# Layer 0's mixed tokens stay in token order, its output projection takes every fourth column as its weights, and one product is issued later

## The chip, the cores and the metric

The kernel runs on one core of one Trainium2 chip. A core has a matrix engine (TensorE, PE in the profile; its weight loads are shown apart, as PEld), three elementwise engines (VectorE or DVE, ScalarE or ACT, GpSimd or POOL), and SyncE (SP), which here only starts DMAs. The engines run side by side and wait for one another through semaphores. The metric is the device time of one execution in microseconds (us), the median over several runs. The kernel before takes 1310.74 us (3 runs, 1310.58 to 1311.07).

## The reference, cut to what matters

Two layers of a decoder, on 1024 tokens of width 1024, in float32:

```
def swa_sink_mixer(h, pos, w_in, sinks):                       # layer 0
    q, k, v, gate = split_cols(h @ w_in, ...)
    o, _ = banded_attention(rope(q), rope(k), v, 127, sinks)
    return o.reshape(B, S, MIX_WIDTH) * jax.nn.silu(gate)

x = x + mixer(rms_norm(x, norm)) @ w_out                       # both layers; then a last rms_norm
```

Layer 1's mixer is the same with three dilated patterns (1, 4 and 16), merged by their softmax denominators. What matters here is `mixer(...) @ w_out` of layer 0: a product of 1024 tokens x 1024 channels with a 1024 x 1024 matrix.

## The kernel before, in words

**Products.** Every float32 operand of a large product is split into two parts, `hi` (rounded) and `lo` (the rest), and three matmuls (hi hi, hi lo, lo hi) stand for one. Activations lie transposed in `ht[0]` (hi, `ht_hi`) and `ht[1]` (lo, `ht_lo`): 128 channels on the partitions, 8 channel tiles `kt`, 1024 tokens in a row of each. For an output block of 128 tokens the 128 token columns of `ht` are the stationary operand (loaded by LDWEIGHTS, PEld) and the weight rows `w_hi`, `w_lo` stream past (MATMUL, PE). In the profile such a matmul reads `j_bank<-w_hi,ht_hi`: the last name is the stationary one.

**Layer 0's tail.** The attention output of three of the four head groups was stored to `mix_dram`; it comes back through SP's queue in six loads into `qk` (three buffers), each 128 channels x 1024 tokens. The last group is still in `xr` (called `ot` in the code). Each of these eight tiles is split: ScalarE copies it into `ht_hi` (`mix_split`, L1473), VectorE subtracts to get `ht_lo` (L1825). Layer 1 wants its tokens by class (token number modulo 4), so in layer 0 this split also reorders: `mixed_from` reads the tile with a step of 4 floats, `mixed_to` writes it as four runs of 256. The last group's two tiles are first multiplied by the softmax coefficients (`end_product`, L1809, whose `qs` operand comes back from DRAM in a DMA) and by the gate (`end_mix`, L1821).

**The output projection** (jobs `("out", layer, c)`) has 8 token blocks k and three column parts c: 384, 256 and 384 columns. Part 0 goes kt by kt over eight PSUM banks (`early_rows`, `later_row`), so that it can begin before all tiles are split; its first two tiles are worked on between the last attention units. Parts 1 and 2 go block by block, 24 matmuls each. Each part and block takes 8 x 3 matmuls, so the projection of layer 0 has 3 x 8 x 24 = 576 matmuls: 384 of 384 columns and 192 of 256. `block_positions` picks the 128 token columns; before, they are contiguous for layer 0, and with a step of 2 for the third pattern of layer 1 (`s.p == 2`).

**Order.** Every engine's program is written out by hand. VectorE's work at the end of a layer comes in this order: the max of the last units, the split of tile 1 (L1825), the stores of probabilities (`empty_turn`, `probs_t<-t_bank`, L792) that TensorE's last `o_bank<-probs_t,v` (L1305) waits for, the store of the attention output (`store_ot`, L1734), the coefficients, then the other splits with the rest of the last group's mixing.

Of the kernel before, what the change touches and what calls it, by code (L numbers as in the profile page):

```python
# [7 lines left out]
F32 = mybir.dt.float32  # L8
F32R = mybir.dt.float32r
I32 = mybir.dt.int32  # L10
ALU = mybir.AluOpType
ACT = mybir.ActivationFunctionType

P = 128
# [101 lines left out]
def columns(job):  # L116
    return out_width(job[2]) if job[0] == "out" else {"qkv": QKV, "gate": R * HD}[job[0]]


def out_width(c):  # L120

    return OUT_AT[c + 1] - OUT_AT[c]
# [17 lines left out]
def half_slot(n, half):  # L140

    return (2 * n + half) % 3
# [90 lines left out]
def by_class(s):  # L233

    return s.layer == 1 and s.p == 0
# [17 lines left out]

def block_positions(view, s, n):

    if s is not None and s.p == 2:
        start = 256 * (n % 4) + n // 4
        return view[:, start:start + 2 * (P - 1) + 1:2]
    return view[:, n * P:(n + 1) * P]
# [9 lines left out]
def filled_from(view, s):  # L269

    return view.rearrange("a (e n i) -> a e n i", e=2, n=NB) if by_class(s) else view


def mixed_to(view, layer):

    return view.rearrange("a (e i) -> a e i", e=4) if layer == 0 else view


def mixed_from(view, layer):

    return view.rearrange("a (i e) -> a e i", e=4) if layer == 0 else view

# [126 lines left out]
def trunk(nc, x, positions, gains, sinks_0, final_norm, w_qkv, w_gate, w_out, out):  # L411
    ctx = ExitStack()
    with ctx:
        def sb(name, shape, dt=F32):
            return ctx.enter_context(nc.sbuf_tensor(name, shape, dt))

        def sem(name):
            return ctx.enter_context(nc.semaphore(name))
# [5 lines left out]
        ht = [sb("ht_hi", [P, KT, S], F32R), sb("ht_lo", [P, KT, S], F32R)]  # L424
# [100 lines left out]
        def gate_of(layer, g):  # L525

            return ot[0] if layer == 0 and g == GROUPS - 1 else gate

        def weights(job, part, kt):

            return w_split[part][:, half_slot(JOB[job], kt // 4), kt % 4, 0:columns(job)]

        def quarter(n, q, part):

            return w_split[part][:, half_slot(n, q // 2), 2 * (q % 2):2 * (q % 2) + 2, 0:columns(JOBS[n])]

        def raw_quarter(n, q):
            return w_raw[:, q % 2, :, 0:columns(JOBS[n])]
# [46 lines left out]
        mix_hi = sem("mix_hi")  # L585
        mix_lo = sem("mix_lo")
# [62 lines left out]
        def groups_before(t):  # L649
            return sum(s.ends_group for s in STEPS[:t])  # L650
# [8 lines left out]
        def sum_links(layer):  # L659

            return 1 if layer == 0 else 5


        def end_links(layers):

            return sum(2 * sum_links(n) + 2 for n in range(layers))
# [13 lines left out]
        def out_region(s):  # L680

            return (s.t - s.p) % 4
# [454 lines left out]
        def _(pe):  # L1137
# [32 lines left out]
            def operands(job, k):  # L1170

                if job[0] == "gate":
                    r, half = k // 2, k % 2
                    return (lambda i, kt: weights(job, i, kt)[:, r * P:(r + 1) * P],
                            lambda i, kt: ht[i][:, kt, half * 512:(half + 1) * 512], 512)
                s = STEPS[job[1]] if job[0] == "qkv" else None
                return (lambda i, kt: block_positions(ht[i][:, kt, :], s, k),
                        lambda i, kt: weights(job, i, kt), columns(job))
# [145 lines left out]
            for layer in (0, 1):  # L1324
# [32 lines left out]
                last = steps[-1]  # L1357
# [26 lines left out]
        def _(act):  # L1384
# [82 lines left out]
            def mix_in_split(layer, k):  # L1467

                act.wait_ge(mix_back[k % 3], 16 * (layer * 2 + k // 3 + 1))
                mix_split(layer, k, mix_in[k % 3])  # L1470

            def mix_split(layer, k, src):
                act.activation(mixed_to(ht[0][:, k, :], layer), mixed_from(src, layer), ACT.Copy).then_inc(mix_hi, 1)  # L1473

            def square(k, n):
                row_ready(k)(act, n)
# [45 lines left out]
            for layer in (0, 1):  # L1522
# [52 lines left out]
                last = steps[-1]  # L1575
# [41 lines left out]
        def _(dve):  # L1617
            def w_lo(quarters):
                for n, q in quarters:
                    if q % 2 == 0:  # L1620
                        dve.wait_ge(w_hi_done, 4 * n + q + 1)
                        dve.tensor_tensor(quarter(n, q, 1), raw_quarter(n, q), quarter(n, q, 0).bitcast(F32),
                                          ALU.subtract).then_inc(w_lo_done["v"], 1)
# [80 lines left out]
            def empty_turn(s, u):  # L1704
                if u % 2 == 1:
                    store_turn(dve, dve.tensor_copy, s, u).then_inc(turn_empty["v"], 1)
# [29 lines left out]
            def link(ins, sem_, value):  # L1736
                ins.then_inc(sem_, 1)
                dve.wait_ge(sem_, value)

            def coefs_first(s, k):  # L1740

                rs = coef_calls(s)[k]
                n = links_before(s.t) + k * links_per_group(s.layer)
                dve.wait_ge(exped, UNITS * s.t + NB * (rs[-1] + 1))
                if groups_before(s.t) > 0:

                    before = [q for q in STEPS[:s.t] if q.ends_group][-1]
                    dve.wait_ge(turned, TURN.filled(("C", before.t, len(coef_calls(before)) - 1)))
                at = comb_of(0, s, rs)
                if s.layer == 0:  # L1750
                    sinks = neg_sink[:, R * s.g + 2 * rs[0]:R * s.g + 2 * rs[-1] + 2]
                    sinks = sinks.rearrange("p (r o j) -> p r o j", o=1, j=2).broadcast_to([P, len(rs), NB, 2])
                    link(dve.tensor_tensor(at[:, :, 0, :, :], stat_of(s, rs, 0, 2), sinks, ALU.subtract), den_v, n + 1)
                    return
                dve.wait_ge(nat_in, 64 * (s.g + 1))
                least = comb_small[:, 0, rs[0]:rs[-1] + 1, :, :]
                link(dve.tensor_tensor(least, nat_of(0, rs, 0, 2), nat_of(1, rs, 0, 2), ALU.min), den_v, n + 1)
                link(dve.tensor_tensor(least, least, stat_of(s, rs, 0, 2), ALU.min), den_v, n + 2)
                for p in range(3):
                    of = stat_of(s, rs, 0, 2) if p == 2 else nat_of(p, rs, 0, 2)  # L1760
                    last = dve.tensor_tensor(at[:, :, p, :, :], least, of, ALU.subtract)
                link(last, den_v, n + 3)
# [37 lines left out]
            def end_product(s, r, p):  # L1800

                dve.wait_ge(ot_stored, 4 * s.t + 2 * r + 2)
                tile, by = ot[(out_region(s) + p) % 4][:, r, :], coef_end[r][p]
                if s.layer == 1:
                    tile = tile.rearrange("a (r i f) -> a f r i", r=4, f=2)
                    by = by.rearrange("p (f n i) -> p f n i", f=2, n=4)
                dve.wait_ge(end_in[3 * r + p], 32 * (1 + (s.layer == 1 and p == 0)))
                done = end_links(s.layer) + r * (sum_links(s.layer) + 1) + max(1, 2 * p)
                link(dve.tensor_tensor(tile, tile, by, ALU.mult), end_mixed, done)  # L1809


            def end_mix(s, r):

                done = end_links(s.layer) + r * (sum_links(s.layer) + 1) + 1
                into = ot[out_region(s)][:, r, :]
                for p in range(1, 1 if s.layer == 0 else 3):
                    end_product(s, r, p)
                    done += 2
                    link(dve.tensor_tensor(into, into, ot[(out_region(s) + p) % 4][:, r, :], ALU.add), end_mixed, done)
                dve.wait_ge(silued, groups_before(s.t) + 1)  # L1820
                link(dve.tensor_tensor(into, into, gate_of(s.layer, s.g)[:, r, :], ALU.mult), end_mixed, done + 1)  # L1821

            def mix_split(layer, k, src):
                dve.wait_ge(mix_hi, layer * (MIX_LOADS + 2) + k + 1)
                dve.tensor_tensor(mixed_to(ht[1][:, k, :], layer), mixed_from(src, layer),  # L1825
                                  mixed_to(ht[0][:, k, :], layer).bitcast(F32), ALU.subtract).then_inc(mix_lo, 1)

            def square(k, n):
                row_ready(k)(dve, n)
# [147 lines left out]
            for layer in (0, 1):  # L1977
# [57 lines left out]
                                coef_copy(s, 0)  # L2035
                last = steps[-1]
                coefs_first(last, 1)
                end_product(last, 0, 0)
                empty_turn(last, UNITS - 1)
                store_ot(last, 1, 1)  # L2040
                coefs_last(last, 1)
                for k in range(2, MIX_LOADS):
                    mix_split(layer, k, mix_in[k % 3])
                    if k == 2:
                        coef_copy(last, 1)
                    if k == 4:
                        w_lo(END_SPLIT[layer])
                        end_mix(last, 0)
                for k in range(2):
                    mix_split(layer, MIX_LOADS + k, ot[out_region(last)][:, k, :])  # L2050
# [82 lines left out]
```

## Time and profile before

| | |
|---|---|
| median of 3 runs | 1310.74 us |
| the profiled execution | 1306.06 us, its span 1304.3 us |
| TensorE busy | 97% of the span, granted clock 0.998 |
| VectorE, ScalarE, GpSimd busy | 59%, 49%, 28% |
| chain that ended last | TensorE 85% (L1162, the products, 59% in `j_bank` alone) |

The page gives for each engine its busy time and share of the span. The chain that ended last is followed back from the last instruction; a line's share of it is what it holds of the path that sets the end. A timeline gives instructions in order of time, with the idle time before one and who ended it. A busy TensorE need not be one at its peak: its instructions overlap, so the pace is read from the starts. Layer 0's tail with its output projection lies at about 341 to 442 us of the span.

### The profile page before, as it was taken

The numbers are of one execution on the slowest core, as the hardware profiler recorded it, in microseconds if no ns is written. First come the engines' busy times: TensorE is split into PE (matmuls) and PEld (weight loads), VectorE is DVE, ScalarE is ACT, GpSimd is POOL, SyncE is SP. The second block draws the span as 40 slices with busy tenths as digits, with TensorE's granted clock in tenths as the row PEclk, the third lists the DMA queues.
The fourth block names the chain that finished last, engine by engine and source line by source line (L and its number), as shares of the span: only waits on it lengthen the run. The fifth ranks groups of instructions, "written<-read, shape, count | busy, mean of one in ns | idle before, by whom it ended". The sixth has DMA issues, their size and how long they took to land.

```text
span 1304.3 us, 24577 instructions
## 1 busy us (share of the span) xinstructions
PE 1268.8 (97%) x8714; PEld 1182.7 (91%) x8714; DVE 763.3 (59%) x2339; ACT 643.5 (49%) x1777; POOL 368.9 (28%) x427
## 2 busy tenths in 40 slices
PE   4999999999999999999999999999999999999997
PEld 4998998988799999999989999899999899987997
DVE  5745453554772545666546666456775466668825
ACT  6445354454751445555446555456554456555312
POOL 2311142140301021212214932215832118610110
PEclk9999999999999999999999999999999999999999
DMA  5101012031546202101112311202310213215723
GB/s 203 39 19 50 26 54 85 18 98 37 173 148 202 98 25 54 40 25 25 51 50 65 86 58 36 65 26 83 98 44 19 65 39 91 84 31 138 212 98 129
DMA packets 101223, 97.29 MB, mean 75 GB/s; under 512 B 30704, under 2 KB 87536, under 8 KB 101104
## 3 DMA queue, kind: packets, MB, share of 16 engines
q1 hardware_dynamic: 101104, 95.73, 24.5%
q8 instruction: 71, 1.16, 0.4%
q14 instruction: 48, 0.39, 0.1%
HBM read 79.46 MB, written 16.25 MB: 73 GB/s over the span
## 4 chain that ended last, share of the span: by engine, by line
PE 85%; DVE 5%; issue 4%; DMA 3%; ACT 1%; SPq 1%; POOL 1%; DVEq 0%; ACTq 0%; POOLq 0%
PE j_bank L1162 59%; PE o_bank L1305 7%; PE t_bank L1284 6%; PE s_bank L1271 5%; PE j_bank L1249 3%; PE s_bank L1273 2%; DMA w_raw<-in_w_qkv 1%; PE o_bank L1162 1%; PE t_bank L1162 1%; DMA gate<-in_positions 1%; PE s_bank L1162 1%; DVE xr L1809 1%; DVE probs L1658 1%; DMA w_raw<-in_w_out 1%; DVE probs L1651 0%
## 5 line engine op out<-in xcount | busy, mean ns | idle before, releaser
L1162 PE MATMUL j_bank<-w_hi,ht_hi 128*128 128x384 f32 (+1 forms) x1312 | 445.0, 339 | 4.3 <-ACT v L1418 2.4
L1162 PE MATMUL j_bank<-w_lo,ht_hi 128*128 128x384 f32 (+1 forms) x1312 | 432.8, 330 | 0.0
L1162 PE MATMUL j_bank<-w_hi,ht_lo 128*128 128x384 f32 (+1 forms) x1312 | 432.7, 330 | 0.0
L1162 PEld LDWEIGHTS j_bank<-w_hi,ht_hi 128*128 128x128 f32 x1312 | 248.5, 189 | 16.2 <-issue 9.5
L1056 POOL TENSOR_TENSOR w_lo<-w_raw,w_hi 128x768 fp32r<-128x768 f32 (+1 forms) x60 | 104.6, 1744 | 550.9 <-ACT w_hi L1395 475.3
L1404 ACT ACTIVATE probs<-probs,stat 128x256 f32<-128x256 f32 (+1 forms) x512 | 231.0, 453 | 48.6 <-DVE stat L1663 46.7
L1162 PEld LDWEIGHTS j_bank<-w_lo,ht_hi 128*128 128x128 f32 x1312 | 248.8, 190 | 0.0
L1162 PEld LDWEIGHTS j_bank<-w_hi,ht_lo 128*128 128x128 f32 x1312 | 248.4, 189 | 0.0
L792 ACT COPY probs_t<-t_bank 128x256 f32<-128x256 f32 (+1 forms) x128 | 58.0, 453 | 282.2 <-PE o_bank L1305 276.5
L1395 ACT ACTIVATE w_hi<-w_raw 128x768 fp32r<-128x768 f32 (+1 forms) x120 | 88.5, 764 | 84.2 <-PE j_bank L1162 42.6
L1305 PE MATMUL o_bank<-probs_t,v 128*64 128x128 f32 x1600 | 116.4, 282 | 1.5 <-DVE probs_t L792 0.9
L1655 DVE CUSTOM_DVE_ANT_0 probs<-s_bank,masks 128x256 f32<-128x256 f32 x224 | 86.1, 421 | 51.6 <-PE t_bank L1284 50.6
L1074 POOL TENSOR_TENSOR rot<-qk,sines 128x96 f32<-128x96 f32 x64 | 28.3, 442 | 295.3 <-DVE v L1682 190.7
L1284 PE MATMUL t_bank<-ident,probs 128*128 128x128 f32 x800 | 109.0, 273 | 1.2 <-ACT probs L1404 1.1
L1305 PEld LDWEIGHTS o_bank<-probs_t,v 128*64 128x64 f32 x1600 | 85.0, 137 | 23.7 <-issue 21.3
L1162 PE MATMUL j_bank<-ht_hi,w_hi 128*128 128x512 f32 x256 | 103.5, 404 | 1.7 <-ACT gate L1422 1.7
L1162 PE MATMUL j_bank<-ht_lo,w_hi 128*128 128x512 f32 x256 | 100.3, 392 | 0.0
L1162 PE MATMUL j_bank<-ht_hi,w_lo 128*128 128x512 f32 x256 | 100.2, 391 | 0.0
L1717 DVE TENSOR_TENSOR qs<-j_bank,qs 64x512 fp32r<-64x512 f32 x118 | 81.3, 689 | 30.2 <-ACT qs L1452 28.4
L1680 DVE COPY qk<-j_bank 128x320 f32<-128x320 f32 x64 | 31.4, 490 | 114.3 <-PE j_bank L1162 114.0
L1404 ACT ACTIVATION_READ_ACCUMULATOR probs<-probs,stat 128x1 f32 x512 | 96.1, 188 | 0.0
L1284 PEld LDWEIGHTS t_bank<-ident,probs 128*128 128x128 f32 x800 | 90.4, 140 | 2.2 <-issue 2.0
(170 smaller groups left out, 1849.4 us busy)
## 6 DMA issues: line engine op xcount, KB each, us to landing
w_raw<-in_w_qkv SPq DMA_DIRECT2D x64, 384.0 KB, 3.5
coef<-coef_dram SPq DMA_DIRECT2D x96, 128.0 KB, 3.0
w_raw<-in_w_gate SPq DMA_DIRECT2D x32, 256.0 KB, 3.3
mix_dram<-xr SPq DMA_DIRECT2D x12, 512.0 KB, 3.9
w_raw<-in_w_out SPq DMA_DIRECT2D x16, 384.0 KB, 3.7
qk<-mix_dram SPq DMA_DIRECT2D x12, 512.0 KB, 5.3
xr<-in_x SPq DMA_DIRECT2D x8, 512.0 KB, 7.2
out<-xr SPq DMA_DIRECT2D x7, 512.0 KB, 2.7
```

What stands on the lines that cost most here:

```text
L792: return copy(to[:, :, lo:2, :], src[:, :, lo:2, :])
L1056: pool.tensor_tensor(quarter(n, q, 1), raw_quarter(n, q), quarter(n, q, 0).bitcast(F32), ALU.subtract).then_inc(w_lo_done["p"], 1)
L1162: last = pe.matmul(to, a(x_, kt), b(y_, kt), start=(start and kt == kts[0] and x_ == y_), stop=(stop and kt == kts[-1] and x_ == 1))
L1249: last = pe.transpose(fill_bank(key)[:, i * P:(i + 1) * P], qk[:, 4 * half + i, c0:c0 + P], ident[:, :])
L1271: last = pe.matmul(to, q, ks[:, part, (n - 1) * P:(n + 1) * P], start=(part == 0), stop=(part == 1))
L1284: last = pe.transpose(t_bank[TURN.bank(key)][:, (2 * j + side) * P:(2 * j + side + 1) * P], probs[:, i % PROBS, j, side, :], ident[:, :])
L1305: last = pe.matmul(o_bank[group % 2][64 * j:64 * j + 64, (n % 4) * P:(n % 4 + 1) * P], v[:, s.t % 2, n - 1 + side, :], probs_t[:, i % 2, 2 ...
L1395: act.activation(quarter(n, q, 0), raw_quarter(n, q), ACT.Copy).then_inc(w_hi_done, 1)
L1404: last = act.activation(row, row, ACT.Exp, bias=stat[:, s.t % 2, n, r, j:j + 1], scale=SCALE, accum_out=stat[:, s.t % 2, n, r, 2 + j:3 + j])
L1655: last = dve.tensor_tensor_reduce(row[:, j, :, :], src[:, j, :, :], mask_of(s, n), 1.0, -BIG, ALU.add, ALU.max, mx[:, i % 2, j:j + 1])
L1680: dve.tensor_copy(qk[:, k, 0:R * HD + HD], src[:, 0:R * HD + HD])
L1717: return dve.tensor_tensor(filled_to(to, s, half), filled_from(at, s), filled_to(of, s, half).bitcast(F32), ALU.subtract)
```

## The change

Three edits, all in layer 0's tail. First, `mix_split` no longer reorders: `ht_hi` and `ht_lo` of the mixed tokens are written in token order, and read in token order, on ScalarE and VectorE. Second, the output projection of layer 0 takes block k as 128 token columns with a step of 4 floats (16 bytes), starting at `512 * (k % 2) + k // 2`, so that its output blocks are the same tokens as before. Layer 1's projection still takes contiguous columns. Third, in layer 0 VectorE's first `end_product` is issued after two splits more and the low parts of a weight piece, right ahead of its `end_mix`, and not ahead of the store of the last unit's probabilities.

```
 def block_positions(view, s, n):
-    if s is not None and s.p == 2:
+    if s is None:
+        start = 512 * (n % 2) + n // 2
+        return view[:, start:start + 4 * (P - 1) + 1:4]
+    if s.p == 2:
         start = 256 * (n % 4) + n // 4
         return view[:, start:start + 2 * (P - 1) + 1:2]
...
-def mixed_to(view, layer):
-    return view.rearrange("a (e i) -> a e i", e=4) if layer == 0 else view
-def mixed_from(view, layer):
-    return view.rearrange("a (i e) -> a e i", e=4) if layer == 0 else view
...
+                if job[0] == "out" and job[1] == 1:
+                    return (lambda i, kt: ht[i][:, kt, k * P:(k + 1) * P], lambda i, kt: weights(job, i, kt), columns(job))
                 s = STEPS[job[1]] if job[0] == "qkv" else None
                 return (lambda i, kt: block_positions(ht[i][:, kt, :], s, k),
                         lambda i, kt: weights(job, i, kt), columns(job))
...
             def mix_split(layer, k, src):          # ScalarE
-                act.activation(mixed_to(ht[0][:, k, :], layer), mixed_from(src, layer), ACT.Copy).then_inc(mix_hi, 1)
+                act.activation(ht[0][:, k, :], src, ACT.Copy).then_inc(mix_hi, 1)
...
             def mix_split(layer, k, src):          # VectorE
-                dve.tensor_tensor(mixed_to(ht[1][:, k, :], layer), mixed_from(src, layer),
-                                  mixed_to(ht[0][:, k, :], layer).bitcast(F32), ALU.subtract).then_inc(mix_lo, 1)
+                dve.tensor_tensor(ht[1][:, k, :], src, ht[0][:, k, :].bitcast(F32), ALU.subtract).then_inc(mix_lo, 1)
...
                 coefs_first(last, 1)
-                end_product(last, 0, 0)
+                if layer == 1:
+                    end_product(last, 0, 0)
                 empty_turn(last, UNITS - 1)
                 store_ot(last, 1, 1)
                 coefs_last(last, 1)
...
                     if k == 4:
                         w_lo(END_SPLIT[layer])
+                        if layer == 0:
+                            end_product(last, 0, 0)
                         end_mix(last, 0)
```

The order of instructions changes on VectorE alone, at one place, the end of layer 0. Before, it reads (the store of the last probabilities is the second `probs_t<-t_bank`, the product is `xr<-xr,qs`):

```order
L1825 TENSOR_TENSOR ht_lo<-qk,ht_hi 128x1024
L792 COPY probs_t<-t_bank 128x512
L1734 COPY xr<-o_bank 128x512
L1753 TENSOR_TENSOR comb<-stat,neg_sink 128x16
L1809 TENSOR_TENSOR xr<-xr,qs 128x1024
L792 COPY probs_t<-t_bank 128x512
L1734 COPY xr<-o_bank 128x512
L1773 TENSOR_TENSOR comb_small<-comb,stat 128x16
L1774 RECIPROCAL comb<-comb_small 128x16
L1825 TENSOR_TENSOR ht_lo<-qk,ht_hi 128x1024
L1798 COPY v<-t_bank 16x128
```

and in the changed kernel the same stretch, whose lines are numbered anew, and with the rest up to the product:

```order
L1748 TENSOR_TENSOR comb<-stat,neg_sink 128x16
L785 COPY probs_t<-t_bank 128x512
L1729 COPY xr<-o_bank 128x512
L1768 TENSOR_TENSOR comb_small<-comb,stat 128x16
L1769 RECIPROCAL comb<-comb_small 128x16
L1820 TENSOR_TENSOR ht_lo<-qk,ht_hi 128x1024
L1793 COPY v<-t_bank 16x128
L1820 TENSOR_TENSOR ht_lo<-qk,ht_hi 128x1024 x2
L1617 TENSOR_TENSOR w_lo<-w_raw,w_hi 128x768
L1804 TENSOR_TENSOR xr<-xr,qs 128x1024
L1816 TENSOR_TENSOR xr<-xr 128x1024
```

The product moved behind eight rows; nothing else changed its place on any engine. What changed on TensorE is the address pattern of 576 weight loads, which the order doesn't show.

## Rows read from the trace of the kernel before

**Rows 1.** The page: busy us, share of the span, instructions; TensorE's granted clock (tenths).
```profile
PE 1268.8 (97%) x8714; PEld 1182.7 (91%) x8714; DVE 763.3 (59%) x2339; ACT 643.5 (49%) x1777; POOL 368.9 (28%) x427
...
PEclk9999999999999999999999999999999999999999
```

**Rows 2.** Stages of the tail: window, its us, each engine's busy us, clock, DMA.
```profile
341.00:375.00 34.00, 31.44 (x221) 28.52 (x221) 28.41 (x43) 25.91 (x33) 6.99 (x5) 1.00 0.46 141
...
389.70:442.00 52.30, 52.30 (x364) 52.27 (x363) 16.62 (x35) 10.84 (x14) 5.57 (x3) 1.00 0.46 156
```

**Rows 3.** Timeline of PE: start us, us, instruction, idle before and who ended it.
```profile
351.41 0.45 PE L1162 MATMUL s_bank<-w_hi,ht_hi 128*128 128x384 f32 x1 [0.74 <-DVE stat L1663]
...
353.34 0.44 PE L1162 MATMUL j_bank<-w_hi,ht_hi 128*128 128x384 f32 x1 [0.61 <-DVE ht_lo L1825]
...
357.89 0.66 PE L1305 MATMUL o_bank<-probs_t,v 128*64 128x128 f32 x8 [0.30 <-ACT probs_t L792]
359.45 0.66 PE L1305 MATMUL o_bank<-probs_t,v 128*64 128x128 f32 x8 [0.90 <-DVE probs_t L792]
```

**Rows 4.** Timeline of DVE, the same stretch.
```profile
346.26 2.68 DVE L1825 TENSOR_TENSOR ht_lo<-qk,ht_hi 128x1024 fp32r<-128x1024 f32 x1
...
351.28 2.01 DVE L1825 TENSOR_TENSOR ht_lo<-qk,ht_hi 128x1024 fp32r<-128x1024 f32 x1
...
357.45 1.23 DVE L1809 TENSOR_TENSOR xr<-xr,qs 128x1024 f32<-128x1024 f32 x1 [2.89 <-DMA qs<-coef_dram]
358.71 0.69 DVE L792 COPY probs_t<-t_bank 128x512 f32<-128x512 f32 x1
...
363.81 3.91 DVE L1825 TENSOR_TENSOR ht_lo<-qk,ht_hi 128x1024 fp32r<-128x1024 f32 x2
...
378.39 1.99 DVE L1825 TENSOR_TENSOR ht_lo<-xr,ht_hi 128x1024 fp32r<-128x1024 f32 x1 [1.40 <-ACT ht_hi L1473]
```

**Rows 5.** Timeline of ACT, three splits in a row.
```profile
357.85 5.96 ACT L1473 ACTIVATE ht_hi<-qk 128x1024 fp32r<-128x1024 f32 x3
```

**Rows 6.** Groups of DVE in layer 1's tail, 1200 to 1240 us: busy, mean ns.
```profile
L1825 DVE TENSOR_TENSOR ht_lo<-qk,ht_hi 128x1024 fp32r<-128x1024 f32 x5 | 6.0, 1217 | 0.1
...
L1809 DVE TENSOR_TENSOR xr<-xr,qs 128x1024 f32<-128x1024 f32 x4 | 4.9, 1220 | 0.1
```

**Rows 7.** Groups of ACT in the same stretch of layer 1.
```profile
L1473 ACT ACTIVATE ht_hi<-qk 128x1024 fp32r<-128x1024 f32 x4 | 4.1, 1056 | 2.2 <-DMA qk<-mix_dram 2.2
```

**Rows 8.** The chain that ended last: start us, us, what; tile 7 begins.
```profile
385.57 1.04 PE j_bank L1162 x6
```

**Rows 9.** Timeline of DVE: blocks of part 1, then of part 2, are emptied.
```profile
398.39 0.42 DVE L1691 TENSOR_TENSOR xr<-j_bank,gate 128x256 f32<-128x256 f32 x1 [2.46 <-PE j_bank L1162]
...
401.27 0.42 DVE L1691 TENSOR_TENSOR xr<-j_bank,gate 128x256 f32<-128x256 f32 x1 [1.59 <-PE j_bank L1162]
...
421.12 0.56 DVE L1691 TENSOR_TENSOR xr<-j_bank,qk 128x384 f32<-128x384 f32 x1 [3.60 <-PE j_bank L1162]
...
425.28 0.56 DVE L1691 TENSOR_TENSOR xr<-j_bank,qk 128x384 f32<-128x384 f32 x1 [2.34 <-PE j_bank L1162]
```

**Rows 10.** Timeline of PEld: two weight loads behind a pause, contiguous columns.
```profile
360.04 0.19 PEld L1162 LDWEIGHTS t_bank<-w_hi,ht_hi 128*128 128x128 f32 x1 [0.17 <-issue]
360.15 0.19 PEld L1162 LDWEIGHTS t_bank<-w_lo,ht_hi 128*128 128x128 f32 x1
```

**Rows 11.** Groups of PEld, 510 to 540 us, contiguous columns.
```profile
L1162 PEld LDWEIGHTS j_bank<-w_lo,ht_hi 128*128 128x128 f32 x26 | 4.9, 188 | 0.0
```

**Rows 12.** The same, 560 to 600 us, columns with a step of 2.
```profile
L1162 PEld LDWEIGHTS j_bank<-w_lo,ht_hi 128*128 128x128 f32 x48 | 9.3, 195 | 0.0
```

**Rows 13.** Timeline of PEld: the first loads of a block with a step of 2.
```profile
580.70 0.20 PEld L1162 LDWEIGHTS j_bank<-w_hi,ht_hi 128*128 128x128 f32 x1
580.82 0.20 PEld L1162 LDWEIGHTS j_bank<-w_lo,ht_hi 128*128 128x128 f32 x1
581.00 0.20 PEld L1162 LDWEIGHTS j_bank<-w_hi,ht_lo 128*128 128x128 f32 x1
```

## The prediction

> **What bounds the kernel now.** I read the page first, then the stages of layer 0's tail, then the timelines of each engine there. TensorE is busy for 97% of the span at the full granted clock, 2.4 GHz, the higher of its two levels [rows 1]. So an edit shortens the kernel only where TensorE stands idle, and lengthens it wherever TensorE's own stream gets slower. The stages say where which holds. From 341 to 375 us TensorE is busy 31.44 of 34.00 us: 2.56 us are idle. From 389.7 us to 442 us, which are parts 1 and 2 of the projection, it is busy all the time, and so are the weight loads [rows 2]. Four idle gaps make up the 2.56 us: 0.74 us for VectorE's max (`stat`), 0.61 us for the split of tile 1, 0.30 us for ScalarE's and 0.90 us for VectorE's store of probabilities, together 2.55 [rows 3].
>
> **The cheap half: shorter splits.** VectorE's split takes 2.01 us where nothing disturbs it, 2.68 at 346.26 us [rows 4]. The same instruction in layer 1, where it reads contiguously, takes 1.22 us [rows 6]. ScalarE's three take 5.96 us, 1.99 each [rows 5], against 1.06 in layer 1 [rows 7]. So the eight splits of layer 0 give back about 8 x 0.8 = 6.4 us of VectorE and 8 x 0.95 = 7.6 us of ScalarE. Little of this is on TensorE's path. The split at 346.26 us ends 1.2 to 1.5 us earlier; everything behind it on VectorE moves with it, so `stat` is ready about 1.3 us earlier, and the gap of 0.74 us closes. The split of tile 1 then begins 1.3 us earlier and lasts 0.8 us less: its gap of 0.61 us closes too. What the later splits save lies under TensorE's work: the last split of layer 0 ends at 378.39 + 1.99 = 380.38 us [rows 4], and TensorE gets to its tile, the eighth, at 385.57 us [rows 8]. No DMA and no queue is moved; SP's fourth to sixth load of `qk` may start earlier, which nobody waits for.
>
> **The product.** Before, VectorE waits 2.89 us for the `qs` DMA, works 1.23 us, and only then stores the last unit's probabilities, for which TensorE waits 0.90 us [rows 3, 4]. With the product behind, this store follows the matmuls before it, as ScalarE's does, and I count the 0.90 us as gone. The product's 1.23 us then stand ahead of the first `end_mix`. Behind it wait the remaining splits, with 5.2 us of slack for the last tile as above, and VectorE has gained 6.4 us on the way; so it costs nothing. ScalarE's gap of 0.30 us stays. Gains: 0.74 + 0.61 + 0.90 = 2.25 us, 2.5 at most with all four gaps, and nothing at least if other waits take their place.
>
> **The dear half: 576 weight loads with a step of 16 bytes.** First the pace now. Part 1's blocks are emptied at 398.39 and 401.27 us: 2.88 us for 24 matmuls of 256 columns, 0.120 us each. Part 2's at 421.12 and 425.28 us: 4.16 us for 24 of 384 columns, 0.173 each [rows 9]. A weight load is hidden as long as it is shorter than that. What does one take? Behind a pause two loads start 0.11 us apart (360.04 and 360.15), so 128 contiguous columns take about 0.107 us; the record of 0.19 us includes latency that overlaps [rows 10]. The 256-column matmuls have therefore almost nothing left to hide a longer load with.
>
> No load with a step of 4 is in this trace. Two things bear on it. One is loads with a step of 2, in layer 1: their mean record is 195 ns instead of 188, their first two starts lie 0.12 us apart instead of 0.11, and the matmuls keep their pace of 0.17 [rows 11, 12, 13]. The other is how the other engines read the same memory. With a step of 8 bytes VectorE's product in layer 1 is as fast as without (1.22 us [rows 6]; `end_product` reads with a step of 2 there, and takes 1.23 contiguously in layer 0 [rows 4]). With 16 bytes, which are the splits of layer 0, both engines fall to one pace although their contiguous paces differ: two splits of VectorE take 3.91 us, so the second adds 3.91 - 2.02 = 1.9 us [rows 4], and of ScalarE's three each takes 1.99 [rows 5], some 1.8 to 1.9 ns an element after the overhead of an instruction. That looks like a limit on the memory's side: about 1.8 ns for each 16 bytes that an element must be fetched from. The loads with a step of 2 fit it: they touch 64 such pieces, 64 x 1.8 = 115 ns, 8 more than 107, and the record grew by 7. With a step of 4 every column is in a piece of its own: 128 x 1.8 = 230 ns. I take 0.235 us for the spacing of a matmul with such a load (an estimate; the matmuls' own overhead beyond the load is not known). Then
>
> - 384 matmuls of 384 columns: 384 x (0.235 - 0.173) = 23.8 us
> - 192 matmuls of 256 columns: 192 x (0.235 - 0.120) = 22.1 us
> - together +45.9 us, less 2.25 us of gaps: +43.7 us.
>
> The bounds. Below, the load stays under 0.120 us as with a step of 2, and costs nothing. A middle value is twice the contiguous load, 0.213 us: 384 x 0.040 + 192 x 0.093 = 33.2 us, net +31. Above, the spacing is the slowest pace of an element, 1.99 us / 1024 = 1.94 ns x 128 = 0.249 us, plus 0.013 us (0.120 less 0.107, what a matmul adds now): 0.262 us, 384 x 0.089 + 192 x 0.142 = 61 us, net +59. I take the value near the line-by-line count, since the rows with a step of 2 lie on it.
>
> The Trainium skill, "SBUF — State Buffer", section "Door 1: The DMA port swizzle", has a note on 16-byte cachelines that speaks both ways. It says that at least two hits in a line are needed for full pace; by that a step of 4 floats, one hit in a line, pays. It also lists 4 fp32 as a step that is free; by that the loads would cost nothing and the sum would be -2.25 us. The splits on VectorE and ScalarE agree with the first sentence (2.01 against 1.22 us) and not with the list; no row here shows TensorE at that step.
>
> **The sum.** Against the profiled execution: 1306.06 + 43.7 = 1349.7 us. That execution lies 4.7 us under the median of the runs; against the median it is 1310.74 + 43.7 = 1354.4, and I say 1354 us.
>
> **The rivals.** (1) TensorE's load path doesn't mind the step: it fetches ahead, and the load stays under 0.120 us. For it: the step of 2 cost the stream nothing, and the path is another one than VectorE's. Against it: the record did grow by 7 ns, by as much as the count of pieces says. Then only the gaps count: 1310.74 - 2.25 = 1308.5 us, 0.17% under before. It decides from a load of 0.120 us downward. (2) The load lies between 0.120 and 0.173 us, under the wide matmuls and over the narrow ones: only part 1 pays, at most 192 x 0.053 = 10.2 us, so 1309 to 1319 us. Nothing in the rows has such a middle pace. (3) The load reads every piece more than once, being of a four-byte type that takes 0.107 us for 128 columns contiguously while a step of 2 still hides that. At 0.30 us: 384 x 0.127 + 192 x 0.18 = 83 us, about 1392 us. The record at a step of 2 speaks against it, since it would have grown more. (4) The engine's clock falls, as TensorE streams less in a time unit. The trace shows no stretch below full clock, so I have no row for it; I put it with (3).
>
> **How the numbers follow.** The forecast, a spacing of 0.21 to 0.26 us, 1338 to 1368 us: 0.80. Rival 1: 0.11. Rival 2: 0.05. Rivals 3 and 4: 0.04. The range 1338 to 1368 leaves out 0.20. A change of 0.2% (2.6 us) is about what a measurement can tell from none. Rival 1 lies just within it, so I give it 0.07 as no change and 0.04 as faster; of rival 2, 0.01 is no change. Slower: 0.80 + 0.04 + 0.04 = 0.88; same 0.08; faster 0.04.
>
> **What would show it.** In the profile after: splits of 1.22 us on VectorE and 1.06 on ScalarE; none of the gaps of 0.74, 0.61 and 0.90 us; the `qs` product right ahead of `xr<-xr`, without a wait. Part 1's blocks are emptied every 5.6 us (24 x 0.235) instead of 2.88, part 2's every 5.6 instead of 4.16: both at the same distance, for the load sets it and not the width. The records of these loads stand near 310 ns (188 + 123). From the first split to the norm of layer 1 (442 us) the stretch is some 44 us longer, and what follows is as long as before. I am wrong if the blocks of part 1 keep 2.88 us (rival 1), if only they get longer (rival 2), or if the granted clock is under full in this stretch.

## The result, and the profile after

The changed kernel takes 1346.84 us (4 runs, 1345.9 to 1348.28) against 1310.66 us before: 36.2 us longer, a ratio of 1.0277 with a 95% interval of 1.0259 to 1.0295. Its profiled execution takes 1346.62 us with a span of 1344.8 us.

The page of the changed kernel (busy us, share, instructions; then the granted clock) shows TensorE and its weight loads both 44 us busier than before [rows 1], with the same number of instructions at the same clock:

```profile
PE 1312.4 (98%) x8714; PEld 1226.9 (91%) x8714; DVE 759.9 (57%) x2339; ACT 636.3 (47%) x1777; POOL 368.7 (27%) x427
...
PEclk9999999999999999999999999999999999999999
```

The stages of the tail (window, its us, busy us of PE, PEld, DVE, ACT, POOL, then the clock). In the first, which answers to that of [rows 2], 0.30 us of TensorE's idle time are left of 2.56. In the second, inside the projection, it is busy all the time:

```profile
341.00:375.00 34.00, 33.70 (x205) 31.69 (x205) 24.26 (x46) 20.18 (x36) 8.93 (x6) 1.00 0.53 160
...
395.00:442.00 47.00, 47.00 (x203) 47.00 (x202) 8.30 (x16) 3.27 (x4) 1.87 (x2) 1.00 0.29 101
```

TensorE's timeline from 346 to 372 us (start, us, instruction, idle before). One of the four gaps of [rows 3] is left, ScalarE's:

```profile
357.37 1.25 PE L1300 MATMUL o_bank<-probs_t,v 128*64 128x128 f32 x16 [0.30 <-ACT probs_t L785]
```

VectorE's timeline. The splits take 1.22 us instead of 2.0 (the first, at 345.37 us, 1.91 instead of 2.68) [rows 4], the store of the last probabilities waits for TensorE and no longer for a DMA, and the product runs later without a wait:

```profile
349.81 1.22 DVE L1820 TENSOR_TENSOR ht_lo<-qk,ht_hi 128x1024 fp32r<-128x1024 f32 x1
...
357.21 0.69 DVE L785 COPY probs_t<-t_bank 128x512 f32<-128x512 f32 x1 [4.90 <-PE o_bank L1300]
...
366.58 1.21 DVE L1804 TENSOR_TENSOR xr<-xr,qs 128x1024 f32<-128x1024 f32 x1
```

So both cheap halves did what they say. The dear one shows where the projection's blocks are emptied, 5.60 us apart in both parts, instead of 2.88 and 4.16 [rows 9]:

```profile
415.05 0.42 DVE L1686 TENSOR_TENSOR xr<-j_bank,gate 128x256 f32<-128x256 f32 x1 [5.17 <-PE j_bank L1155]
...
420.65 0.42 DVE L1686 TENSOR_TENSOR xr<-j_bank,gate 128x256 f32<-128x256 f32 x1 [4.31 <-PE j_bank L1155]
...
448.71 0.56 DVE L1686 TENSOR_TENSOR xr<-j_bank,qk 128x384 f32<-128x384 f32 x1 [5.24 <-PE j_bank L1155]
...
454.31 0.56 DVE L1686 TENSOR_TENSOR xr<-j_bank,qk 128x384 f32<-128x384 f32 x1 [5.04 <-PE j_bank L1155]
```

5.60 / 24 = 0.2333 us a matmul, whatever its width; part 0's matmuls, 384 columns wide, start 0.233 us apart as well (ten such steps from 384.80 to 387.13 us). The groups of weight loads from 400 to 440 us (mean ns behind the busy time) have records of 330 ns, against 188 to 190 for contiguous and 195 for every second column [rows 11, 12]:

```profile
L1155 PEld LDWEIGHTS j_bank<-w_hi,ht_lo 128*128 128x128 f32 x58 | 19.1, 330 | 0.0
```

By these paces the loads cost 384 x (0.2333 - 0.1733) + 192 x (0.2333 - 0.120) = 23.0 + 21.8 = 44.8 us. That is 8.6 us more than the medians differ by. Where those come back is what the first experiments ask.

### The profile page after: what moved, and what is told of

Its sections match the earlier page's. It is cut to its first block, busy times and chain, and to the rows that moved or that the text cites. A ratio compares the mean times of both kernels' runs of the same rounds, so it can differ in the third digit from the quotient of the medians.

```text
span 1344.8 us, 24578 instructions
## 1 busy us (share of the span) xinstructions
PE 1312.4 (98%) x8714; PEld 1226.9 (91%) x8714; DVE 759.9 (57%) x2339; ACT 636.3 (47%) x1777; POOL 368.7 (27%) x427
## 4 chain that ended last, share of the span: by engine, by line
PE 67%; DVE 4%; ACT 2%; issue 1%; DMA 1%; SPq 0%; POOL 0%; DVEq 0%; ACTq 0%
PE j_bank L1155 46%; PE o_bank L1300 6%; PE t_bank L1279 5%; PE s_bank L1266 3%; PE j_bank L1244 2%; PE s_bank L1268 2%; PE s_bank L1155 1%; PE o_bank L1155 1%; PE t_bank L1155 1%; DMA w_raw<-in_w_qkv 1%; ACT probs L1399 1%; DMA w_raw<-in_w_out 0%; DVE xr L1804 0%; DVE xr L1871 0%; DVE probs L1653 0%
## 5 line engine op out<-in xcount | busy, mean ns | idle before, releaser
L1155 PE MATMUL j_bank<-w_hi,ht_hi 128*128 128x384 f32 (+1 forms) x1312 | 457.2, 348 | 3.9 <-ACT v L1413 2.9
L1155 PE MATMUL j_bank<-w_lo,ht_hi 128*128 128x384 f32 (+1 forms) x1312 | 444.8, 339 | 0.0
L1155 PE MATMUL j_bank<-w_hi,ht_lo 128*128 128x384 f32 (+1 forms) x1312 | 444.8, 339 | 0.0
L1155 PEld LDWEIGHTS j_bank<-w_hi,ht_hi 128*128 128x128 f32 x1312 | 268.7, 205 | 15.5 <-issue 9.3
L1155 PEld LDWEIGHTS j_bank<-w_lo,ht_hi 128*128 128x128 f32 x1312 | 269.0, 205 | 0.0
L1155 PEld LDWEIGHTS j_bank<-w_hi,ht_lo 128*128 128x128 f32 x1312 | 268.7, 205 | 0.0
```

What stands on the lines that cost most here:

```text
L1155: last = pe.matmul(to, a(x_, kt), b(y_, kt), start=(start and kt == kts[0] and x_ == y_), stop=(stop and kt == kts[-1] and x_ == 1))
```

## The experiments

The reference time of "before" below is that of the same chip session: 1308.58 us (26 runs, 1303.56 to 1311.81) for the first four, 1309.93 (15 runs) for the next four, 1307.97 (18 runs, 1303.27 to 1313.5) for the last. The last session ran on another chip. The changed kernel was timed only beside the 1310.66 us of the result, so every difference to its 1346.84 us below is one between sessions; the medians of before differ by up to 2.7 us between them.

### Two steps of two instead of one of four

The class of a token is taken in two halves: the splits read every second token, and the loads take every second column. Nothing then has a step of 16 bytes.

```
 def block_positions(view, s, n):
     if s is None:
-        start = 512 * (n % 2) + n // 2
-        return view[:, start:start + 4 * (P - 1) + 1:4]
+        start = 512 * (n // 2 % 2) + 256 * (n % 2) + n // 4
+        return view[:, start:start + 2 * (P - 1) + 1:2]
...
+def mixed_to(view, layer):
+    return view.rearrange("a (e i) -> a e i", e=2) if layer == 0 else view
+def mixed_from(view, layer):
+    return view.rearrange("a (i e) -> a e i", e=2) if layer == 0 else view
```

> The change with its step of 4 taken in two steps of 2: the splits on ScalarE and VectorE read every second token and write two runs of 512, and the projection's weight loads take every second column; the product stays late. Theory (a load costs one fetch of about 1.8 ns for each 16-byte piece it touches, so a step of 2 hides in 0.120 us and the gain on VectorE remains): matmuls at 0.120 and 0.173 us, splits of 1.22 us on VectorE, no gaps of 0.74, 0.61 and 0.90 us; 2.25 us under the kernel before, about 1308.4 us. Rival (any strided load costs TensorE): over 1320 us. Rival (the gaps only hid other waits): 1310.7 us.

Measured: 1302.12 us (12 runs, 1301.35 to 1302.82), ratio to before 0.9955 (0.9943 to 0.9968). It beats both kernels: 6.5 us under before, 44.7 under the change. Matmuls keep 0.120 us: part 1's blocks of this kernel are emptied 2.88 us apart,

```profile
393.06 0.43 DVE L1696 TENSOR_TENSOR xr<-j_bank,gate 128x256 f32<-128x256 f32 x1 [2.46 <-PE j_bank L1165]
395.94 0.42 DVE L1696 TENSOR_TENSOR xr<-j_bank,gate 128x256 f32<-128x256 f32 x1 [2.46 <-PE j_bank L1165]
```

and its VectorE's splits take 1.23 us although they read with a step of 8 bytes:

```profile
359.07 1.23 DVE L1830 TENSOR_TENSOR ht_lo<-qk,ht_hi 128x1024 fp32r<-128x1024 f32 x1
```

The mechanism holds, and the size doesn't: 2.25 us were expected and 6.5 came.

### The change with contiguous loads

```
-        start = 512 * (n % 2) + n // 2
-        return view[:, start:start + 4 * (P - 1) + 1:4]
+        return view[:, n * P:(n + 1) * P]
```

> The changed kernel with only the loads of layer 0's projection made contiguous again; it leaves out the regrouping of layer 0's tokens by class. Theory (the whole loss is the step of the loads): matmuls at 0.120 and 0.173 us, 1308.4 us, that is 38 us under the changed kernel and 2.25 us under the one before. Rival (a part of the loss is the late product or the earlier DMAs): over 1311 us.

Measured: 1302.01 us (9 runs, 1300.56 to 1302.66), 0.9956 of before (0.9941 to 0.9971). Against the changed kernel these are 1346.84 - 1302.01 = 44.8 us, the sum of the paces; that the two agree to 0.1 us is partly luck, as the sessions differ. The step of the loads is the whole loss, and the other two edits are worth 6.6 us (1308.58 - 1302.01), not 2.25.

### Only the product moved

The kernel before with its first `end_product` of layer 0 moved as in the change.

> The kernel before with the product moved late and nothing else. Theory: the gap of 0.90 us closes, those of 0.74 and 0.61 stay; about 1309.8 us (0.9 under before). Rival (the product late delays the last tiles, since the splits still take 2.0 us each): 1310.7 us or over, with a wait of TensorE for ht_lo after 380 us.

Measured: 1303.28 us (12 runs, 1302.67 to 1305.28), 0.9968 of before (0.9953 to 0.9983). The move alone gives 5.3 us where the trace had 0.90. The splits' share is what is left to 1302.1: 1.2 us, near the two gaps of 0.74 and 0.61. This profiled execution names a suspect. Among SP's DMA issues in it the coefficients' (`qs`) stands at 355.48 us; in the profiled execution of before it stood at 351.66:

```profile
351.34 0.80 SPq L889 DMA_DIRECT2D mix_dram<-xr  x2
352.19 0.78 SPq L840 DMA_DIRECT2D coef_dram<-v  x1
355.48 1.26 SPq L872 DMA_DIRECT2D qs<-coef_dram  x2
```

With the product late nobody notices. With it early VectorE would have stood still until some 361 us (an estimate: in the first profile of before the product started 5.8 us behind that issue). So the theory became: the DMA's arrival varies from one execution to the next, and the one execution profiled first was an early one.

### The change with the product early

```
-                if layer == 1:
-                    end_product(last, 0, 0)
+                end_product(last, 0, 0)
...
-                        if layer == 0:
-                            end_product(last, 0, 0)
```

> The changed kernel with the product early again, as before. Theory: the loads set the pace (0.233 us a matmul) and TensorE waits 0.5 to 0.9 us for the store of the last probabilities: 1347 to 1348 us, at most 1 us over the changed kernel. Rival (slower matmuls ahead of it cover the wait for the DMA): the same as the changed kernel, 1346.8 us.

Measured: 1352.76 us (5 runs, 1347.4 to 1353.92). Neither expectation holds: it is 5.9 us over the changed kernel. The profiled execution is the fastest of the five at 1347.4 us, and TensorE waits only 0.31 us for the store in it. The other four are 5.2 to 6.5 us slower. A profile showed the lucky case once more.

### The product early, on data at hand

The kernel before, with the first factor taken from the tile itself, so that the product waits for no DMA; the wait stands at the late place.

```
+                if s.layer == 0 and r == 0:
+                    by = tile
+                else:
+                    dve.wait_ge(end_in[3 * r + p], 32 * (1 + (s.layer == 1 and p == 0)))
...
+                        if layer == 0:
+                            dve.wait_ge(end_in[0], 32)
                         end_mix(last, 0)
```

> The kernel before, product early, but its second operand is data at hand (the tile itself) instead of the coefficients in qs; the wait for their DMA stands where the late product would be. It leaves out the coefficients of one tile. Theory (what the early product costs is the wait for a DMA whose arrival varies by some 4 us between executions, not its own 1.2 us): about 1303.5 us, as with the product late, and a spread of 2 or 3 us as there instead of 8. Rival (the product's own work or its place costs the 5 us): 1308 us, with the spread of the kernel before.

Measured: 1303.72 us (6 runs, 1302.66 to 1304.62), 0.9956 of its before (0.9943 to 0.997). The product's own 1.2 us at the early place cost nothing to speak of. The wait behind which everything else of VectorE queued cost the 5 to 6 us, and the spread.

### The kernel before, profiled twice more

> The kernel before once more, for another profiled execution of it. Theory (the coefficients' DMA arrives at times that differ by some 4 us, and with the product early VectorE passes the delay on to TensorE): if this execution takes about 1310 us, the wait for qs is some 6 to 7 us instead of 2.9 and TensorE's wait for the last probabilities some 5 us instead of 0.9; if it takes about 1306 us, both are as in the first profile. Rival (the slower executions lose their time elsewhere): 1310 us with waits of 2.9 and 0.9 us.

> A third profiled execution of the kernel before, with the same expectations as the second: its time and TensorE's wait for the last probabilities rise and fall together.

Measured: 1310.36 and 1309.46 us, one execution each. VectorE's product and TensorE's wait in the second profile (1310.36 us):

```profile
360.01 1.23 DVE L1809 TENSOR_TENSOR xr<-xr,qs 128x1024 f32<-128x1024 f32 x1 [5.65 <-DMA qs<-coef_dram]
```

```profile
362.02 1.12 PE L1305 MATMUL o_bank<-probs_t,v 128*64 128x128 f32 x8 [3.64 <-DVE probs_t L792]
363.07 0.69 PE L1162 MATMUL t_bank<-w_hi,ht_hi 128*128 128x384 f32 x1
363.55 0.52 PE L1162 MATMUL t_bank<-w_lo,ht_hi 128*128 128x384 f32 x1
363.87 0.52 PE L1162 MATMUL t_bank<-w_hi,ht_lo 128*128 128x384 f32 x1
```

and the same two of the third profile (1309.46 us):

```profile
359.69 1.23 DVE L1809 TENSOR_TENSOR xr<-xr,qs 128x1024 f32<-128x1024 f32 x1 [4.64 <-DMA qs<-coef_dram]
```

```profile
361.70 0.66 PE L1305 MATMUL o_bank<-probs_t,v 128*64 128x128 f32 x8 [2.67 <-DVE probs_t L792]
```

Three executions of one kernel: TensorE's wait is 0.90, 2.67 and 3.64 us, its time 1306.06, 1309.46 and 1310.36 us. The waits grow by 1.8 and 2.7, the times by 3.4 and 4.3: there is more to it than the wait. The windows of the second profile around it show what (the number before the last two is the granted clock):

```profile
355.00:361.00 6.00, 3.07 (x35) 2.38 (x34) 0.99 (x1) 2.63 (x3) 1.32 (x1) 0.95 0.79 242
361.00:362.00 1.00, 0.00 (x0) 0.00 (x0) 0.93 (x2) 0.94 (x1) 0.00 (x0) 0.50 0.37 135
...
364.00:366.00 2.00, 2.00 (x8) 2.00 (x7) 1.85 (x2) 1.98 (x2) 0.00 (x0) 0.50 0.00 0
366.00:370.00 4.00, 4.00 (x21) 3.91 (x21) 1.92 (x3) 2.26 (x2) 0.00 (x0) 0.85 0.01 2
```

From 360.4 us, inside the wait, the clock is granted at 0.50, the lower level of 1.2 GHz, until 367.2 us, and the matmuls stand 0.32 us apart (363.55 and 363.87 above) instead of 0.173. Some twelve of them at 0.147 us more are 1.8 us, and the eight of `o_bank` take 1.12 instead of 0.66. Wait and clock together make 2.7 + 1.8 + 0.5 = 5.0 us, less 0.5 because its gap for `stat` was 0.24 us instead of 0.74: 4.5 for the 4.3 measured. In the first profile the clock stays at 1.00 through this stretch, its longest wait here being 0.90 us. In the third profile the clock is still at 1.00 when the wait ends at 361.70 us; it falls 1.2 us later, and for 3.4 us:

```profile
362.00:364.00 2.00, 2.00 (x15) 1.81 (x11) 1.42 (x4) 2.00 (x2) 0.00 (x0) 0.72 0.00 0
364.00:366.00 2.00, 2.00 (x8) 2.00 (x7) 1.65 (x1) 1.98 (x2) 0.00 (x0) 0.50 0.04 8
```

The runs without a profile fit this. Over the 59 executions of before in the three sessions, the four with a mean granted clock of 0.999 took 1303.56 to 1304.71 us, the eleven with 0.994 took 1309.29 to 1311.81 us.

All three profiles of before, the first too, have a second such place, at the end of layer 1's attention. TensorE waits there 0.94 to 0.95 us for `stat`, and the clock is then granted at 0.50 for 3.4 us. The first profile:

```profile
1183.94 0.51 PE L1273 MATMUL s_bank<-ks,qs 128*128 128x256 f32 x2 [0.94 <-DVE stat L1663]
```

```profile
1184.00:1186.00 2.00, 1.72 (x12) 1.26 (x14) 1.93 (x9) 0.80 (x4) 0.00 (x0) 0.78 1.04 422
1186.00:1188.00 2.00, 2.00 (x10) 1.38 (x7) 1.83 (x12) 1.84 (x9) 0.00 (x0) 0.50 0.61 240
1188.00:1190.00 2.00, 2.00 (x9) 1.64 (x8) 1.49 (x10) 0.27 (x3) 0.00 (x0) 0.86 0.00 0
```

The lower clock costs some 1.5 us there: from TensorE's transposes right behind this wait (1184.94 us) to its next gap for `stat` (1202.57 us) it takes 17.63 us, against 16.12 us in the profile of the two steps of two (1182.28 to 1198.40 us). In the nine profiles of kernels whose product is late or waits for no DMA, the changed kernel's among them, this wait is 0.58 or 0.59 us and the clock stays at 1.00. In the profiles of the two other kernels whose early product waits for the DMA the wait is 0.94 and 0.95 us, and the clock stays at 1.00 too. So a part of what the edits give back comes from layer 1, where the prediction had nothing. Why the wait is longer in all five profiles in which the early product waits for the DMA, and why the clock falls behind it in three of them and not in two, stays open.

The expectation had named waits of 6 to 7 us for `qs` and of some 5 us for TensorE: they were 5.65 and 3.64, the rest was the clock. Why the coefficients come late is shown only in part. In the second profile the `mix_dram` store starts at 349.86 us, in the first at 347.12, 2.7 us later, and the `qs` DMA behind it in SP's order starts 2.9 us later. Of this, 1.6 us are GpSimd's last multiply ahead of the store (2.85 us against 1.29), and 1.2 us a later start of GpSimd's four multiplies (342.86 against 341.69 us). In the fourteen profiles of this case the `qs` DMA starts between 351.66 and 355.48 us. The first profile of before has the earliest of these starts, and that of the change with the product early, the fast one of its five, the next (351.90). Why GpSimd is later and slower in some executions wasn't tried.

### Two steps of two, with the product early

> The step of 4 in two steps of 2, with the product early. Theory: the splits' gaps (0.74 and 0.61 us) are closed, the wait for the DMA is not, and since all else comes 1 to 2 us earlier it weighs more: 5 to 7 us over the same with the product late, 1307 to 1309 us. Rival (shorter splits alone give the gain): 1303 us.

Measured: 1309.05 us (12 runs, 1303.23 to 1310.82), 1.0002 of before (0.9986 to 1.0019). With the product early the shorter splits are worth nothing in the median: TensorE gets to the same wait earlier and waits longer. In this kernel's profile (1308.6 us) the wait is 4.11 us:

```profile
361.89 1.12 PE L1310 MATMUL o_bank<-probs_t,v 128*64 128x128 f32 x8 [4.11 <-DVE probs_t L795]
```

### Other steps of the loads

The same line, with a step of 3 (`start = 80 * n`), with a step of 8 in parts 0 and 1 (`start = n`), and with the step of 4 in part 1 alone.

> The changed kernel with the projection's loads at a step of 3 floats (12 bytes); other tokens are then multiplied. Theory (a load costs one fetch for each 16-byte piece it touches): 128 columns touch 96 pieces, 0.171 to 0.175 us a load; both widths at 0.175, so 192 x 0.055 = 10.6 us over the version with contiguous loads, about 1312.6 us. Rival (a threshold at 16 bytes, anything less is free): 0.120 and 0.173, 1302 us. Rival (every step of over 8 bytes costs as much as 16): 0.233, 1347 us.

> The changed kernel with parts 0 and 1 of layer 0's projection at a step of 8 floats (32 bytes) and part 2 contiguous; other tokens are then multiplied. Theory (pieces touched): a step of 8 touches 128 pieces like a step of 4, so 0.233 us a matmul in parts 0 and 1: 192 x 0.060 + 192 x 0.113 = 33.2 us over the version with contiguous loads, 1335 us. Rival (the cost grows with the distance): 0.3 us or more a matmul in these parts, over 1360 us.

> The changed kernel with the step of 4 kept in part 1 alone (192 matmuls of 256 columns), parts 0 and 2 contiguous; the tokens of these are in another order. Theory: part 1 alone costs 192 x (0.233 - 0.120) = 21.8 us, 1323.8 us. Rival (the cost is spread alike over all 576 matmuls, 45 us / 576 = 0.078 us each): 15 us, 1317 us.

Measured: 1314.53 us (6 runs), 1338.35 us (2 runs) and 1323.03 us (2 runs). The emptying of part 1's blocks with a step of 3, 4.17 us apart (0.174 a matmul):

```profile
409.33 0.42 DVE L1686 TENSOR_TENSOR xr<-j_bank,gate 128x256 f32<-128x256 f32 x1 [3.74 <-PE j_bank L1155]
413.50 0.42 DVE L1686 TENSOR_TENSOR xr<-j_bank,gate 128x256 f32<-128x256 f32 x1 [3.74 <-PE j_bank L1155]
```

and with a step of 8, 5.80 us apart (0.242):

```profile
411.44 0.42 DVE L1685 TENSOR_TENSOR xr<-j_bank,gate 128x256 f32<-128x256 f32 x1 [5.38 <-PE j_bank L1154]
417.24 0.42 DVE L1685 TENSOR_TENSOR xr<-j_bank,gate 128x256 f32<-128x256 f32 x1 [5.38 <-PE j_bank L1154]
```

| step of the loads | 16-byte pieces touched | us a matmul, 256 columns | load's record, ns |
|---|---|---|---|
| 1 | 32 | 0.120 | 188 to 190 |
| 2 | 64 | 0.120 | 195 to 196 |
| 3 | 96 | 0.174 | 258 |
| 4 | 128 | 0.233 | 330 |
| 8 | 128 | 0.242 | 338 |

The pace follows the pieces touched, 1.81 to 1.82 ns each at steps 3 and 4; a step of 8, twice the distance with as many pieces, adds only 4% to one of 4. Steps of 5 to 7 weren't tried. Neither "free below 16 bytes" nor "dear above 8" holds. Two sums were off, for reasons that the rows show. At a step of 3 the wide matmuls stood 0.178 us apart too (4.28 us a block), which adds some 1.9 us to 1312.6. At a step of 8 the measured pace gives 192 x (0.242 - 0.173) + 192 x (0.242 - 0.120) = 36.6 us over 1302.0, that is 1338.6. Part 1 alone at a step of 4 cost 1323.03 - 1302.01 = 21.0 us, for 21.8 expected from the width, and not 15.

### The product late in layer 1 as well

> Two steps of 2, and the product late in layer 1 as well. Theory: in layer 1 the first product waits for nothing in the trace and TensorE's wait for the stores is under 0.5 us, so at most that is gained; VectorE's chain to the last split is as long as before: 1301.7 to 1302.1 us. Rival (layer 1 hides the same varying wait): 1298 us. Rival (the product late delays layer 1's last tiles): over 1303 us.

Measured: 1302.80 us (7 runs, 1302.43 to 1303.91), 0.9958 of before (0.9942 to 0.9974), against 1302.12 in the other session for the same with layer 1 left alone. No gain. In its profile TensorE now waits 1.69 us for a late split of layer 1, where the version without this edit has a gap of 0.44 us:

```profile
1231.79 0.41 PE L1165 MATMUL j_bank<-w_hi,ht_hi 128*128 128x384 f32 x1 [1.69 <-DVE ht_lo L1830]
```

In layer 1 VectorE has three products to do for each tile, and putting one of them off would delay the tiles; that this is the reason is read from the order of its program and not tried by itself. The best kernel found is the first experiment's.

## Why the prediction was right, point by point

**The dear half** was right in mechanism and size: +45.9 us forecast from a spacing of 0.235 us, 44.8 measured from 0.2333, and 44.8 again as the difference, between two sessions, of two kernels that differ in these loads alone. The count of 16-byte pieces, read from VectorE's and ScalarE's splits and from the 7 ns that a step of 2 added, carried over to TensorE; the steps of 3 and 8 agree with the count. The record was forecast near 310 ns and was 330. The rows show 0.11 us between two contiguous loads and not the third digit of the 0.107 from which the prediction worked.

**The Trainium skill's note** ("SBUF — State Buffer", section "Door 1: The DMA port swizzle"), taken as two hits in a line for full pace, agrees: steps of 1 and 2 have at least two and are hidden (0.120 us a matmul), steps of 4 and 8 have one and pay (0.233 and 0.242). Its list, by which 4 fp32 are free, does not: 0.233 us against 0.120.

**The shorter splits** were right: 1.22 us each but for the first, both gaps gone, 1.2 us of time for the 1.35 forecast (1303.3 less 1302.1), once the product is late.

**The product** is the term that was mis-sized. The step that failed reads "I count the 0.90 us as gone": a gap of one execution was taken as the kernel's. It is worth 5.3 us in the medians (5.9 between the changed kernel and its version with the product early), because the wait for `qs` was longer in both later profiles and the lower clock came with it. The 1.5 us of lower clock in layer 1, present in all three profiles of before and in none of the others, are likely in these numbers as well; no run separates them. The prediction itself noted that the profiled execution lay 4.7 us under the median and left that unexplained; the two later profiles, 3.4 and 4.3 us over the first, show where such microseconds go. With 6.6 us in place of 2.25 the sum is 44.8 - 6.6 = 38.2 us; 36.2 were measured against that session's before, of 4 runs, none of them short, 38.3 against the 26 runs of the next. So of the 7.5 us by which the forecast of 43.7 was too high, 4.4 are this term, 1.1 are the loads, and the other 2.1 are the 4 runs of before, whose median lies that much over that of the 26. The range from 1338 to 1368 us was wide enough to hold all three.

**The bounds** "2.5 at most with all four gaps" were too narrow for the same reason. The rivals on the loads (no cost, only the narrow ones, more than one fetch) all fell. The fourth, a falling clock, didn't come from the slower stream: with loads every 0.233 us the clock stayed at 1.00. It came, unforeseen, in the kernel before, around a wait. The prediction's reason for having no row for it, that the trace shows no stretch below full clock, was a misreading: the page's line has only nines, but the windows from 1184 to 1190 us of the same trace have 0.78, 0.50 and 0.86.

## What to carry to other kernels

In this kernel, weight loads whose 4-byte columns stand 16 bytes or more apart set TensorE's pace at 256 and at 384 columns a matmul; at 12 bytes they set it at 256 and just about at 384. Split such a reordering into two steps of 8 bytes, one where the tile is written and one where it is loaded: both were free here. An instruction that waits for a DMA should not stand ahead of work that TensorE waits for, even if the profile shows a short wait: compare the profiled execution with the median first, and where they differ, profile again before pricing the wait. And look at the granted clock by windows of 2 us: 3.4 us at half the clock vanish in a page that shows the span in 40 slices.

## What the runs showed of the hardware that was not expected

- At step 3 (96 pieces) a load of 128 four-byte columns sets a pace of 0.174 us, at step 4 (128 pieces) 0.233, at step 8 (128 pieces) 0.242: in proportion to the pieces touched in the first two, then nearly flat.
- Waits of TensorE of 3.64 and 4.11 us came with 6.8 us at the granted clock of 0.50, which began inside the wait; one of 2.67 us was followed, 1.2 us behind its end, by 3.4 us of it. Matmuls of 384 columns stood 0.32 us apart meanwhile. In layer 1, waits of 0.94 and 0.95 us were followed by 3.4 us at 0.50 in three profiles and by none in two, so the length of the wait alone doesn't decide.
- Between executions of one kernel a DMA issued behind GpSimd's work started up to 3 us later (351.66, 354.59 and 354.69 us in the three profiles of before). With nothing on the path waiting for it the spread of the runs was 1.5 to 2.6 us, against 6.4 to 10.2 us for before.
